# First keys and queries of latent attention loaded in the stage before it, and opening scores in three more PSUM banks

## The reference

```python
u = h @ w_in
cq, ckv, kr, gate = jnp.split(u, [Q_LORA, Q_LORA + KV_LORA, Q_LORA + KV_LORA + ROPE_DIM], axis=-1)
q = (rms_norm(cq, g_q) @ w_uq)      # 8 heads, 128 plain + 64 rotary columns
kv = (rms_norm(ckv, g_kv) @ w_ukv)  # 8 heads, 128 key + 128 value columns
q_rope, kr = rope_2d(q_rope, tables), rope_2d(kr, tables)      # latent tokens only
...
s = jnp.einsum('bhqd,bhkd->bhqk', qi, k).astype(jnp.float32) * scale   # keys: 2048 + 256
p = jax.nn.softmax(s, axis=-1).astype(v.dtype)
return jnp.einsum('bhqk,bhkd->bhqd', p, v)
```

## Time and profile before

| | |
|---|---|
| median of 3 runs | 3082.19 us (3082.03 to 3082.55) |
| the profiled execution, its own time | 3082.16 us |
| its span, first to last instruction | 3080.3 us |
| PE busy with matmuls | 2920.8 us, 95% of the span |
| weight loads of PE | 2433.6 us, 79% |
| DVE, ACT, POOL busy | 1816.3, 1444.0, 432.5 us |
| mean granted TensorE clock | 0.988 of full speed |
| HBM traffic | 211.85 MB read, 97.66 MB written |

### The profile page before, as it was taken

One profiled execution on the slowest core, in us unless ns is written; L12 is line 12 of the kernel. 1 busy time (PEld: TensorE's weight loads), 2 busy tenths in 40 slices (PEclk: granted clock), 3 DMA queues, 4 the chain that ended last, 5 costly groups with the idle time before them and its releaser, 6 DMA issues. The chain is left out here.

```text
span 3080.3 us, 44414 instructions
## 1 busy us (share of the span) xinstructions
PE 2920.8 (95%) x14789; PEld 2433.6 (79%) x14789; DVE 1816.3 (59%) x3147; ACT 1444.0 (47%) x3071; POOL 432.5 (14%) x493
## 2 busy tenths in 40 slices
PE   2999999869999999999999999999899999999798
PEld 2877878758888887878788888878788888888687
DVE  6545545256777676766677677653444444445875
ACT  2544545345655565655556565534532222122553
POOL 1000000012212222122222222200001111112000
PEclk9999999989999999999999999999999999999899
DMA  6455464541111112121111111135432222222563
GB/s 220 165 183 201 158 213 137 176 130 35 48 57 58 58 33 62 42 73 36 44 57 58 58 32 52 59 130 185 168 117 70 78 71 73 68 72 82 171 199 129
DMA packets 222417, 312.38 MB, mean 101 GB/s; under 512 B 81376, under 2 KB 143088, under 8 KB 221040
## 3 DMA queue, kind: packets, MB, share of 16 engines
q1 hardware_dynamic: 217584, 301.18, 30.3%
q10 hardware_dynamic: 4608, 8.39, 0.7%
HBM read 211.85 MB, written 97.66 MB: 100 GB/s over the span
## 5 line engine op out<-in xcount | busy, mean ns | idle before, releaser
L1155 DVE TENSOR_TENSOR at_ptlo<-at_T,at_pthi 128x512 fp32r<-128x512 f32 x576 | 396.7, 689 | 320.9 <-ACT at_pthi L1028 317.5
L1012 ACT ACTIVATE at_prob<-at_S,at_nmax 128x512 f32<-128x512 f32 (+1 forms) x640 | 410.9, 658 | 368.3 <-DVE at_nmax L1131 353.2
L1028 ACT ACTIVATE at_pthi<-at_T 128x512 fp32r<-128x512 f32 x576 | 348.6, 608 | 212.6 <-PE at_T L897 212.5
L1120 DVE TENSOR_REDUCE at_mx<-at_S 128x1 f32<-128x512 f32 (+1 forms) x640 | 393.9, 631 | 75.0 <-PE at_S L872 52.8
L897 PE MATMUL at_T<-ident,at_prob 128*128 128x128 f32 x2304 | 346.3, 273 | 4.1 <-DVE at_ptlo L1155 4.1
L897 PEld LDWEIGHTS at_T<-ident,at_prob 128*128 128x128 f32 x2304 | 278.6, 140 | 70.4 <-DVE at_ptlo L1155 14.5
L136 PE MATMUL ci_ps<-h1hi,ci_whi 128*128 128x512 f32 x768 | 300.7, 391 | 5.3 <-DVE h1lo L1820 5.3
L137 PE MATMUL ci_ps<-h1lo,ci_whi 128*128 128x512 f32 x768 | 300.3, 391 | 0.0
L138 PE MATMUL ci_ps<-h1hi,ci_wlo 128*128 128x512 f32 x768 | 299.9, 390 | 0.0
L867 PE MATMUL at_S<-at_khi,at_qhi 128*128 128x512 f32 (+1 forms) x640 | 249.7, 390 | 47.8 <-ACT at_prob L1012 24.9
L136 PE MATMUL at_O<-at_pthi,at_vhi 128*128 128x512 f32 x576 | 270.7, 470 | 1.3 <-issue 0.6
(11 more groups left out here) (230 smaller groups left out, 6106.5 us busy)
## 6 DMA issues: line engine op xcount, KB each, us to landing
fr_w<-in_w_front SPq DMA_DIRECT2D x75, 512.0 KB, 4.1
at_wmod<-in_w_mod SPq DMA_DIRECT2D x32, 512.0 KB, 3.4
cv_w<-in_cv_w_in SPq DMA_DIRECT2D x24, 512.0 KB, 4.3
fr_w<-in_w_front SPq DMA_DIRECT2D x24, 384.0 KB, 4.0
values<-fr_ob SPq DMA_DIRECT2D x36, 256.0 KB, 3.0
at_kst<-k_nope SPq DMA_DIRECT2D x8, 1152.0 KB, 7.0
at_vst<-values SPq DMA_DIRECT2D x8, 1152.0 KB, 8.3
fr_x<-in_x SPq DMA_DIRECT2D x16, 512.0 KB, 6.1
```

The lines of the kernel that those rows point to most:

```text
L1012: nc.scalar.activation(prob[:, j % 2, i, k], S[:, c, 0:k.stop - k.start], ACT.Exp, scale=SCALE, bias=nmax[:, i % 2:i % 2 + 1], accum_out=l ...
L1028: nc.scalar.activation(dst, T[:, (n + SLOTS * j) % 2], ACT.Copy).then_inc(s_hi, 1)
L1120: nc.vector.tensor_reduce(mx[:, i % 2, c:c + 1], S[:, c, 0:k.stop - k.start], AXX, ALU.max).then_inc(s_mx, 1)
L1155: nc.vector.tensor_tensor(ptlo[:, kt % 3], T[:, (n + SLOTS * j) % 2], pthi[:, kt % 3].bitcast(F32), ALU.subtract).then_inc(s_lo, 1)
```

## The change

1. `load_first`, `first_high`, `first_low`: the rotary keys, head 0's keys and the first 512 queries are loaded by SP inside `front`, in the turn of `U0` of the last tile behind the stores of `V1`, after waits for the stores that wrote them. Their high halves are made by ACT and their low halves by DVE in the turns of `U3`, `G5` and `U4` (rotary keys, keys, queries). The same loads and splits at the start of `attention` are gone.
2. To have room, `front`'s buffers are arranged anew: the hidden state of the even tiles and of the context, the input tile and the condition rows lie together, and the homes of the keys and queries (57,344 bytes a partition from 110592 on) lie over them when they are spent. Buffers of `attention` and `attn_out` move accordingly, without another order of work.
3. `front` no longer ends with the wait for its last stores to `values`, `silu_gate`, `k_nope` and `q_nope`; SP waits for them in `attention`, behind the load of the second block's queries.
4. In the opening, sub-tiles 1 and 3 put their chunks 0, 1 and 2 in `T[0]`, `T[1]` and `O` instead of `S[0..2]`; chunks 0 to 2 of a sub-tile then wait for the exponentials of two sub-tiles before, chunks 3 and 4 still for those of the sub-tile before. The first transposes and the first values wait until the exponentials of sub-tile 3 have read these banks.

The diff, cut to its core:

```diff
+FIRST_AT = ("U3", "G5", "U4")
...
+def load_first(nc, net, sp):
+
+    sp.dma_start(net.kr_raw[:], net.kr).then_inc(net.s_krin, 16)
+    sp.dma_start(net.k_raw[:], net.kn[0]).then_inc(net.s_k, 16)
+    sp.dma_start(net.qst[:, 0], net.qn[0, :, 0:BLK]).then_inc(net.s_q[0], 16)
+    for half in range(2):
+        sp.dma_start(net.qrst[half * ROPE:(half + 1) * ROPE, 0], net.qr_heads[0, :, 0:BLK]).then_inc(net.s_q[0], 16)
...
+def first_high(nc, net, act, step):
+
+    if step == 0:
+        act.wait_ge(net.s_krin, 16)
+        nc.scalar.activation(net.krhi[:], net.kr_raw[:], ACT.Copy).then_inc(net.s_krhi, 1)
+    if step == 1:
+        act.wait_ge(net.s_k, 16)
+        for c in range(NCHUNK):
+            nc.scalar.activation(net.khi[:, chunk(c)], net.k_raw[:, chunk(c)], ACT.Copy).then_inc(net.s_khi, 1)
+    if step == 2:
+        act.wait_ge(net.s_q[0], 48)
+        nc.scalar.activation(net.qhi[:, 0], net.qst[:, 0], ACT.Copy).then_inc(net.s_qhi, 1)
+        nc.scalar.activation(net.qr_hl[:, 0], net.qrst[:, 0], ACT.Copy).then_inc(net.s_qhi, 1)
...
@@ front, SP
                 if g:
                     stores(g - 1)
+                if t == LAST and name == "U0":
+                    stored = ob_of[out_at(t, "G3")]
+                    for k in range(4):
+                        sp.wait_ge(s_st[k], 16 * len(range(k, stored, 4)))
+                    for u in (5 * (t - 1), 5 * t):
+                        sp.wait_ge(s_rst[u % 2], 16 * (u // 2 + 1))
+                    sp.wait_ge(s_kr, 16)
+                    load_first(nc, net, sp)
             stores(NG - 1)
-            for k in range(4):
-                sp.wait_ge(s_st[k], 16 * len(range(k, NOB, 4)))
+            net.front_stores = [16 * len(range(k, NOB, 4)) for k in range(4)]
...
@@ front, ACT (and the same with first_low on DVE)
+                if t == LAST and name in FIRST_AT:
+                    first_high(nc, net, act, FIRST_AT.index(name))
...
@@ attention
+        def opening(h, j):
+            return isinstance(h, int) and index(h, j) == 0
+
+        def bank(h, j, i, c):
+
+            if opening(h, j) and i % 2 and c < 3:
+                return (T[:, 0], T[:, 1], O[:])[c]
+            return S[:, c]
...
@@ attention, SP
-            load_q(sp, 0, 0)
-            load_k(sp, 0)
-
-            sp.dma_start(prob[:, 1, 0], net.kr).then_inc(s_krin, 16)
+            load_q(sp, 0, 1)
+            for k in range(4):
+                sp.wait_ge(s_st[k], net.front_stores[k])
             load_v(sp, 0)
-            load_q(sp, 0, 1)
...
@@ attention, PE, scores
-                if not (isinstance(t, int) and t == 0):
+                if opening(h, j) and c < 3:
+                    if i >= 2:
+                        pe.wait_ge(s_exp, (i - 2) * NCHUNK + (c + 1))
+                elif not (isinstance(t, int) and t == 0):
                     pe.wait_ge(s_exp, (t - 1) * NCHUNK + (c + 1))
...
@@ attention, ACT
-            act.wait_ge(s_krin, 16)
-            nc.scalar.activation(krhi[:], prob[:, 1, 0], ACT.Copy).then_inc(s_krhi, 1)
-            q_high(0, 0)
-            for c in range(NCHUNK):
-                k_high(0, c)
```

More of the change, by code:

```diff
@@ L98, in placed, with first_low @@
         return st.enter_context(nc.sbuf_tensor(name, shape, dtype))
+def load_first(nc, net, sp):
[16 more added lines that the diff above has]
+        nc.scalar.activation(net.qr_hl[:, 0], net.qrst[:, 0], ACT.Copy).then_inc(net.s_qhi, 1)
+def first_low(nc, net, dve, step):
+    if step == 0:
+        dve.wait_ge(net.s_krhi, 1)
+        nc.vector.tensor_tensor(net.krlo[:], net.kr_raw[:], net.krhi[:].bitcast(F32), ALU.subtract).then_inc(net.s_kr, 1)
+    if step == 1:
+        for c in range(NCHUNK):
+            dve.wait_ge(net.s_khi, c + 1)
+            nc.vector.tensor_tensor(net.klo[:, chunk(c)], net.k_raw[:, chunk(c)], net.khi[:, chunk(c)].bitcast(F32),
+                                    ALU.subtract).then_inc(net.s_klo, 1)
+    if step == 2:
+        dve.wait_ge(net.s_qhi, 2)
+        nc.vector.tensor_tensor(net.qlo[:, 0], net.qst[:, 0], net.qhi[:, 0].bitcast(F32), ALU.subtract)
+        nc.vector.tensor_tensor(net.qr_hl[ROPE:P, 0], net.qrst[ROPE:P, 0], net.qr_hl[ROPE:P, 0].bitcast(F32),
+                                ALU.subtract).then_inc(net.s_qlo, 1)
 def load_heads(nc, net, sp, p):
@@ L208, in front @@
         lat = sb("lat", [P, MR * D])
+        rs = sb("rs", [P, 2, BLK])
+        ob = sb("ob", [P, 4, BLK])
+        xt = sb("x", [P, R, D])
+        h0hi, h0lo = (sb(n, [P, KD, BLK], F32R) for n in ("h0hi", "h0lo"))
+        cb = sb("cb", [P, 2, D])
+        hhi, hlo = (h0hi, h1hi), (h0lo, h1lo)
         raw = lat[:, 0:6 * BLK].rearrange("p (m n) -> p m n", m=6)
@@ L562, in split_hidden @@
                 n, w = b * KD + k, tiles * P
-                hi, lo = (t[:, b % 2, k, 0:w] for t in (hhi, hlo))
+                hi, lo = (t[b % 2][:, k, 0:w] for t in (hhi, hlo))
                 dve.wait_ge(s_h, n + 1)
@@ L682, in _ @@
                         latent_low(t, "c")
+                if t == LAST and name in FIRST_AT:
+                    first_low(nc, net, dve, FIRST_AT.index(name))
                 for o, (kind, i, e, w, ctx) in enumerate(outs[g], first_out[g]):
@@ L885, in transposes @@
                         pe.wait_ge(s_lo, (b if n >= 2 else b - 1) * NKT + before)
+                if opening(h, j) and n == 1:
+                    pe.wait_ge(s_exp, (QT - 1) * NCHUNK + 2)
                 out = T[:, m % 2]
@@ L907, in values @@
                     pe.wait_ge(s_vlo, h * VC + (kt // KPV + 1))
-                if kt == 0 and not (isinstance(b, int) and b == 0):
-                    pe.wait_ge(s_og, b)
+                if kt == 0:
+                    if opening(h, j):
+                        pe.wait_ge(s_exp, (QT - 1) * NCHUNK + 3)
+                    else:
+                        pe.wait_ge(s_og, b)
                 pe.wait_ge(s_lo, b * NKT + (kt + 1))
@@ L1011, in exponential @@
                 k = chunk(c)
-                nc.scalar.activation(prob[:, j % 2, i, k], S[:, c, 0:k.stop - k.start], ACT.Exp, scale=SCALE,
+                nc.scalar.activation(prob[:, j % 2, i, k], bank(h, j, i, c)[:, 0:k.stop - k.start], ACT.Exp, scale=SCALE,
                                      bias=nmax[:, i % 2:i % 2 + 1],
@@ L1119, in maximum @@
                 k = chunk(c)
-                nc.vector.tensor_reduce(mx[:, i % 2, c:c + 1], S[:, c, 0:k.stop - k.start], AXX,
+                nc.vector.tensor_reduce(mx[:, i % 2, c:c + 1], bank(h, j, i, c)[:, 0:k.stop - k.start], AXX,
                                         ALU.max).then_inc(s_mx, 1)
@@ L1209, in _ @@
             nc.vector.memset(ones[:].bitcast(F32), 1.0).then_inc(s_ones, 1)
-            dve.wait_ge(s_krhi, 1)
-            nc.vector.tensor_tensor(krlo[:], prob[:, 1, 0], krhi[:].bitcast(F32), ALU.subtract).then_inc(s_kr, 1)
-            q_low(0, 0)
-            for c in range(NCHUNK):
-                k_low(0, c)
             for i in range(QT):
```

54 lines of the change are left out of this document (32 added, 22 removed).

## The result

The changed kernel took 3063.57 us, median of 4 runs (3061.58 to 3065.63), the kernel before on the same chip 3082.11 (3081.79 to 3082.55): a ratio of 0.994, 95% interval 0.9923 to 0.9957, or some 18.5 us less. Forecast was 3062.6. The profiled execution took 3061.76 (span 3059.9), 20.4 less than that of before; it is the second fastest of the four. The first view shows where: two windows of the profile after, with length, busy time of PE, PEld, DVE, ACT and POOL, granted clock, DMA share and GB/s.

What follows compares the result with a forecast made beforehand. The bound was the 57.5 us from the last front matmul to the steady rhythm. Terms 4.5 + 2.3 + 27.7 + 3.4 = 37.9, so 19.6 less than 3082.16: 3062.6 us, 8 in 10 within 3056 to 3067.

Steps and rivals of the forecast that it cites:

- The opening at full clock: First score to steady rhythm: 27.7 us, with idle banks removing early pauses and a 3.8 us pause inside sub-tile 3.
- The hand-over: Last front-stage matmul to first attention score: PE idle 2.3 us in place of 22.8; bounds 2.2 and 4.3.
- The rival in which the last store is still waited for: At the hand-over, the barrier still waits for the last store or the new block starts slower: 3064.6 us; chance 0.08.
- The hold-up of the front stage: U2's weights queue behind the early loads, delaying DVE's rotations and G5's weights: G5 starts 4.5 us later.
- The clock: Two half-clock spells, at the opening's start and behind its 3.8 us pause, 1.7 us each: 3.4; bounds 0 and 6.
- The splits hide: Front stage, U3, G5 and U4 turns: the ACT and DVE splits cost 0, with 1.6 us to spare.
- the double stall: Splits on ACT delay stores and the loads of G6 and G7; front stage loses 8 to 11: 3066 to 3069; chance 0.12.
- Nothing behind the rhythm: After the steady rhythm starts, the old order of work just shifts; no new wait expected.
- Slower than before: Front stage: new loads run at 115 GB/s or less, sharing engines with stores: 3079.6 us, 3092 at 80; chance 0.03.

Runs made afterwards that it cites:

- the second profile: The unaltered changed kernel run and profiled again, beside the kernel before on the same chip; 3064.47 us, ratio 0.9939.
- The kernel in pieces: Changed kernel with early loads in eleven pieces from G3 to G5, splits two turns later, DVE's second-block query low halves behind sub-tile 2; 3055.65 us, ratio 0.9914.
- low queries later: Changed kernel with DVE's low half of the second block's queries moved from behind sub-tile 1 to behind sub-tile 2; 3058.02 us, ratio 0.9918.
- the loads in three: Changed kernel with the five early loads spread: rotary keys at G3's turn, keys at K1's, queries at V0's; 3064.71 us, ratio 0.994.

## Why the prediction was right, and which of its steps were not

**The opening at full clock: right to 0.1 us.** Forecast from the first score: chunk 3 of sub-tiles 1, 2 and 3 at 9.2, 14.95 and 23.9, the rhythm at 27.7. Measured: 9.09, 14.84, 23.80 and 27.63. The pause before sub-tile 1's chunk 3 was to be 0.6 to 0.8 and is 0.29, since PE came there at 8.8 and not at 8.5; what ends it was right.

**The hand-over: right, 0.3 short.** 2.61 us instead of 2.3. SP's last issue ended at 614.86, 0.98 after the last matmul as forecast, but PE started 1.62 later, not 1.3 as at the other hand-over. It waited for the little DVE write to `at_ones` behind the barrier. The rival in which the last store is still waited for is out, and putting the wait back shows what it costs.

**The hold-up of the front stage: the mis-sized term.** Forecast 4.5 (the chain gave 3.8 to 5.1, the bounds went to 7), measured 7.3 in the first profile and 5.6 in the second. Of the 7.3, 5.7 stand at `G5`: marker to `G5` 78.93 us against 581.77 - 508.56 = 73.21. Its steps: `U2`'s weights in by 572.73 instead of 571.9; the low half done at 574.56 instead of 573.6; the rotations took 5.3 as forecast; from the issue of `G5`'s weights to `G5` 587.53 - 580.31 = 7.2, towards the upper end of 6.2 to 7.5. So each step erred by less than 1 us and to the same side. A likely reason for the first is that I let the 3.28 MB run at the keys' rate as if alone, though stores share the engines; no run shows it apart. The other 1.6 us are the clock: behind the pause of 2.32 PE ran at 0.63 a matmul, and from `G5` to the end it took 26.35 us where it took 24.77 before. Such a spell stood only in the bounds of the clock's term. The mechanism was right but incomplete: the store of a rotation behind the same block would have held DVE nearly as long by itself, to 64.9 us after the marker instead of 65.9.

**The clock: right in number, wrong in place.** I put two spells of half clock, 3.4 us, in the opening. In the first profile the opening has none, though its hand-over pause is 2.61 and its later one 3.52. One stands at `G5`, and the other just behind the rhythm's start, where a window of after has

```profile
646.00:648.00 2.00, 2.00 (x7) 1.60 (x6) 0.81 (x1) 2.00 (x5) 0.00 (x0) 0.50 0.00 0
```

That one costs nothing. Before the change PE ran at full clock there and then stood still, in its timeline:

```profile
670.19 0.66 PE L897 MATMUL at_T<-ident,at_prob 128*128 128x128 f32 x4 [1.59 <-DVE at_ptlo L1155]
```

Now it runs slowly and has no such pause. In the second profile two spells lie in the opening, as forecast, and it takes 30.7. So the sum of the first profile came right in part by luck, by two errors that cancel: 2.8 too little in the front stage, 3.4 too much in the opening. With 5.6, 2.6 and 30.7 the second comes to 38.9 us against my 37.9, by nearly the forecast terms.

**The splits hide: right.** `G6` and `G7` show no pause, as the sum had it; the double stall is out. The kernel in pieces, in which they moved two turns later, shows a wait there, 1.7 us at `G6`, with late weights and a split in it.

**Nothing behind the rhythm: right.** At the start of the rhythm the change is ahead by 664.03 - 644.11 = 19.9 us, at the hand-over from attention to the output projection by 2023.73 - 2003.54 = 20.2, at the end by 20.4.

**Slower than before: out.** It needed loads at 115 GB/s or less. The 3.28 MB took 572.73 - 560.72 = 12.0 us, some 273 GB/s.

## What to carry to other kernels

A load that is moved ahead is paid for by all that stands behind it in its queue, stores included: follow the buffer whose store must land as you follow the weights, and if two chains end at the same engine, freeing one brings nothing. Cut the load into pieces of the size of the stage's own transfers and put them at turns with slack; that took the hold-up from 5 to 7 us down to 2. Look at what an engine does out of turn at a start-up: two rows of DVE work put one sub-tile later gave 6 us by the medians, 4.8 by the profiles, a quarter or more of what the whole change gave.

## What the hardware showed that I had not expected

- **The length of a pause doesn't tell whether the clock falls.** At `G5`, after a dense stage, it fell behind 2.32 us (first profile: 0.63 a matmul) and not behind 2.62 us (low queries later: 0.40). At the hand-over it kept the full clock behind 2.61 in the first profile, and in the second it fell 1.5 us after the first score (617.71), in the midst of dense matmuls. With the loads in three it fell at once, behind 2.62 (614.17: 0.64). Behind 2.38 us at the other hand-over it fell again, as in the earlier trace rows. What decides it stays open; a spell should be priced as a chance (some 1.6 us each, nothing where a wait behind it hides it) and not as a term.
- **An engine stood 4.80 us for a buffer whose store was issued** behind 2.9 MB of loads of the same queue; behind 1.18 MB it stood 4.22.
- **Two microseconds of waiting cost nearly four** (3064.47 to 3068.25). The pause itself explains 2.2; the clock was at half from the first score on, and both spells of the opening lasted longer (11 and 12 matmuls of 512 columns instead of 7 and 5).
